# Gated DeltaNet inverse in a one-core transformer kernel: five doubling levels on TensorE against 16-row diagonal blocks on VectorE, through DRAM, and two levels

## The chip, the cores and the metric

The kernel runs on one core of one Trainium2 chip. The metric is the device time of one execution in microseconds; three runs of the kernel before are given. One more execution was taken by the hardware profiler, and every view below comes from it.

## What is computed

A block of a transformer on 256 tokens of width 2048 in float32: an input projection feeds two mixers, sparse attention and a Gated DeltaNet (GDN), which are gated and merged; an MLP, a second attention layer and a retention layer follow. The change is in the GDN. It has 8 heads of 128, and works on chunks of 64 tokens:

```
lower = where(strict, einsum('bhncd,bhnsd->bhncs', kb, k) * decay, 0)   # c = 64
tinv = triangular_solve(eye + lower, eye, lower=True, unit_diagonal=True)
u = tinv @ vb
w = tinv @ (kb * exp(g))
qk = einsum('bhncd,bhnsd->bhncs', q, k) * decay
# scan over the chunks
v_new = u_n - w_n @ state
o = (q_n * exp(g_n)) @ state + qk_n @ v_new
```

tinv is the inverse of a unit lower triangular 64 x 64 matrix, for 8 heads and 4 chunks.

## The kernel before

**The stream.** Nearly all time goes into projections. A job multiplies the 256 x 2048 activations with a 2048 x 512 block of weights, in 8 granules of 256 weight rows. Weights and activations are split into two float32r parts: ScalarE rounds a granule to w_hi (`split_hi`, L261), VectorE forms the rest, w_lo (`split_lo`, L269), TensorE does 8 matmuls with w_hi (L294) and 4 with w_lo (L300) on 512 columns. w_hi and w_lo have four slots each: `split_hi` of granule r waits until granule r - 4 is done. SyncE loads the weights 512 KB at a time into eight half-slots of raw, ahead of that.

**The slots.** The small work of the GDN is written as one generator per engine (`gdn_mix`), each cut into steps by `yield`. Before granule r, TensorE takes its next step; ScalarE and VectorE take theirs before they split granule r + 4. So step s of every engine lies beside granule s, and a step that waits holds back everything behind it on its engine, the splits too. Group 0 (heads 0 to 3) and group 1 (heads 4 to 7) follow one another, from the fifth GDN job (J_GDN + 4) on; up to the merge projections' end there are 12 jobs, 96 slots. A group takes 36 of them.

**The steps of a group.** On TensorE: 0 to 2 transpose the projected q, k and v of the group to columns; 3 and 4 the cumulated decay; 5 turns k back (`natural(0)`); 7 multiplies k with k; 11 transposes the tiles of A (L1608), 12 turns q (`natural(1)`, L1561); 13 to 22 are the levels of the inverse; 23 and 24 the products w (L1648) and u (L1654); 25 to 31 the scan over four chunks (L1666 to L1683); 35 turns the output (L340), for which VectorE's L2247 makes the last factor. VectorE does the taps of the convolution (`tap`, L2115, four instructions of 256 columns each), the decay matrix, at step 9 A = k k^T times decay and beta (L2166, semaphore a_ready), at step 10 the decay for q k^T and the gate z (L2169, L2172).

**The inverse.** All tiles have 128 x 128 elements, two chunks on the diagonal; 4 heads and 2 tiles make 8 tiles, processed by one instruction on VectorE and ScalarE (1024 columns) and eight on TensorE. Y is the transposed inverse of the diagonal blocks, which double in size at every level. Level 0 is Y = I - mask(0) * A^T (transposes L1608, then VectorE L2175 and L2177). Each of the levels 1 to 5 takes two slots:

```
P  = A^T Y  per tile    TensorE L1618, then transposes of Y, L1626
P1 = P * mask(l)        VectorE L2183;  X = copy of Y^T, ScalarE L1080
U  = X^T P1             TensorE L1633
Y  = Y - U              VectorE L2191
```

The k.q product (L1639) lies in the second slot of level 1, the turn of v (`natural(2)`) in that of level 5. The three taps of v's convolution are beside levels 2 to 4 on VectorE. A 128 x 128 float32 matmul has two records in the trace, a transpose one.

**GpSimd (POOL)** in this stretch only computes three reciprocal roots per group for the norms (`root_pool`, L429), of k, q and the output; it has loaded the masks before, and its other DMAs lie before or after the GDN. Its DMAs go through the queue q0; those of SyncE through q1.

**Memory.** The working tiles lie in one arena; g_nat, the projected heads in rows, is reused for the first four merge gates (`mg_a`), which ScalarE writes with a sigmoid at the end of each merge job.

## Time and profile before

| | us |
|---|---|
| runs (3) | 2828.3, 2831.04, 2833.46 |
| median | 2831.04 |
| profiled execution | 2830.05 |
| its span | 2828.2 |
| granted TensorE clock, mean | 0.995 |
| TensorE busy | 2781.5 |
| VectorE busy | 1606.9 |
| ScalarE busy | 1294.8 |
| GpSimd busy | 65.2 |

The span goes from the first to the last instruction of the profiled execution; some 2 us lie around it. PE is TensorE, PEld its weight loads, DVE is VectorE, ACT ScalarE, POOL GpSimd, SP SyncE. Times in timelines are microseconds from the start of the span. A matmul's duration overlaps the next one's, so the pitch of starts is what it costs.

### The profile page before, as it was taken

Reading aid. Unit: us, or ns where it says so; the run is one execution under the profiler, and the core shown is the slowest. Engines: PE = TensorE matmul, PEld = TensorE weight load, DVE = VectorE, ACT = ScalarE, POOL = GpSimd, SP = SyncE. Lnnn points to the kernel's source line nnn. Section 1 sums busy time; section 2 is a strip of 40 time slices with the busy share of each in tenths; the row PEclk is TensorE's granted clock in tenths of the full one; section 3 lists DMA queues with packets and bytes.
Section 4 is the critical chain, followed back from the end, with each engine's and each line's share of the span. In section 5 each row is a group of like instructions: output and inputs, shape, how many; then the busy total and the mean of one; then the engine's idle time right before and its main releaser. Section 6 shows DMA issues by size and latency. Waiting matters only on the chain.

```text
span 2828.2 us, 35643 instructions
## 1 busy us (share of the span) xinstructions
PE 2781.5 (98%) x13270; PEld 2316.4 (82%) x13270; DVE 1606.9 (57%) x1784; ACT 1294.8 (46%) x1606; POOL 65.2 (2%) x68
## 2 busy tenths in 40 slices
PE   8999999999999999999999999999999999999998
PEld 7878887888888888888888888888878888888887
DVE  5555757555655555555555656655565555555556
ACT  5554636444444444344444554445453434444442
POOL 1000000000000000000000000000000000000000
PEclk9999999999999999999999999999999999999999
DMA  8754534356667566666666587586655655666663
GB/s 240 243 164 142 148 105 138 115 151 193 208 203 193 189 195 185 190 190 187 193 186 186 164 163 171 170 161 161 217 171 169 191 168 188 196 175 183 177 211 123
DMA packets 259947, 502.23 MB, mean 178 GB/s; under 512 B 15880, under 2 KB 24360, under 8 KB 258784
## 3 DMA queue, kind: packets, MB, share of 16 engines
q1 hardware_dynamic: 256448, 486.73, 59.4%
q0 software_dynamic: 3200, 13.52, 1.9%
q8 instruction: 97, 1.59, 0.2%
q14 instruction: 42, 0.34, 0.0%
q10 hardware_dynamic: 160, 0.04, 0.0%
HBM read 496.56 MB, written 3.67 MB: 177 GB/s over the span
## 4 chain that ended last, share of the span: by engine, by line
PE 94%; DVE 2%; ACT 2%; issue 1%; DMA 0%; POOL 0%; ACTq 0%; DVEq 0%
PE acc L294 53%; PE acc L300 27%; PE mx L340 1%; PE acc L1734 1%; PE acc L1732 1%; PE acc L1733 1%; ACT w_hi L261 1%; ACT arena L503 1%; DVE w_lo L269 1%; PE mx L1618 1%; PE mx L1633 1%; PE mx L476 0%; PE mx L484 0%; PE mx L1626 0%; DMA res<-in_x 0%
## 5 line engine op out<-in xcount | busy, mean ns | idle before, releaser
L269 DVE TENSOR_TENSOR w_lo<-raw,w_hi 128x1024 fp32r<-128x1024 f32 x916 | 1123.5, 1228 | 1122.8 <-ACT w_hi L261 1109.7
L261 ACT ACTIVATE w_hi<-raw 128x1024 fp32r<-128x1024 f32 x916 | 971.1, 1061 | 1378.5 <-PE acc L300 1306.1
L294 PE MATMUL acc<-w_hi,lt_b_hi 128*128 128x512 f32 x1792 | 707.3, 395 | 0.0
L294 PE MATMUL acc<-w_hi,lt_b_lo 128*128 128x512 f32 x1792 | 698.0, 390 | 0.0
L294 PE MATMUL acc<-w_hi,lt_a_hi 128*128 128x512 f32 x1664 | 660.2, 397 | 0.0
L294 PE MATMUL acc<-w_hi,lt_a_lo 128*128 128x512 f32 x1664 | 651.1, 391 | 0.0
L300 PE MATMUL acc<-w_lo,lt_b_hi 128*128 128x512 f32 x1792 | 479.3, 389 | 0.0
L300 PE MATMUL acc<-w_lo,lt_a_hi 128*128 128x512 f32 x1664 | 446.8, 390 | 0.8 <-DVE w_lo L269 0.8
L294 PEld LDWEIGHTS acc<-w_hi,lt_b_lo 128*128 128x128 f32 x1792 | 337.0, 188 | 69.8 <-issue 1.9
L300 PEld LDWEIGHTS acc<-w_lo,lt_b_hi 128*128 128x128 f32 x1792 | 336.4, 188 | 70.3
L294 PEld LDWEIGHTS acc<-w_hi,lt_b_hi 128*128 128x128 f32 x1792 | 336.8, 188 | 69.7 <-issue 1.9
L300 PEld LDWEIGHTS acc<-w_lo,lt_a_hi 128*128 128x128 f32 x1664 | 313.6, 188 | 67.2 <-DVE w_lo L269 1.2
L294 PEld LDWEIGHTS acc<-w_hi,lt_a_hi 128*128 128x128 f32 x1664 | 314.2, 189 | 64.5 <-issue 1.0
L294 PEld LDWEIGHTS acc<-w_hi,lt_a_lo 128*128 128x128 f32 x1664 | 314.4, 189 | 62.8
L356 DVE TENSOR_TENSOR lt_a_lo<-mx,lt_a_hi 128x512 fp32r<-128x512 f32 (+1 forms) x64 | 41.2, 685 | 33.8 <-ACT lt_a_hi L348 33.8
L429 POOL TENSOR_TENSOR sm<-sm 128x2 f32<-128x2 f32 (+2 forms) x20 | 23.1, 1154 | 1610.6 <-DVE sm L423 825.0
L348 ACT ACTIVATE lt_a_hi<-mx 128x512 fp32r<-128x512 f32 (+1 forms) x64 | 34.7, 593 | 52.0 <-PE mx L340 52.0
L1732 PE MATMUL acc<-w_hi,lt_b_hi 128*128 128x512 f32 x128 | 50.1, 391 | 0.0
L1734 PE MATMUL acc<-w_hi,lt_b_lo 128*128 128x512 f32 x128 | 49.8, 389 | 0.0
L1733 PE MATMUL acc<-w_lo,lt_b_hi 128*128 128x512 f32 x128 | 49.8, 389 | 0.0
L340 PE MATMUL mx<-ident,arena 128*128 128x128 f32 x280 | 36.4, 273 | 2.9 <-DVE arena L2247 2.9
L340 PEld LDWEIGHTS mx<-ident,arena 128*128 128x128 f32 x280 | 32.5, 140 | 8.1 <-DVE arena L2247 3.8
(378 smaller groups left out, 1627.0 us busy)
## 6 DMA issues: line engine op xcount, KB each, us to landing
raw<-in_ret_w_in SPq DMA_DIRECT2D x192, 512.0 KB, 3.7
raw<-in_w_in SPq DMA_DIRECT2D x168, 512.0 KB, 3.6
raw<-in_w_up SPq DMA_DIRECT2D x128, 512.0 KB, 3.7
raw<-in_w_down SPq DMA_DIRECT2D x128, 512.0 KB, 4.5
raw<-in_fox_w_in SPq DMA_DIRECT2D x128, 512.0 KB, 4.5
raw<-in_ret_w_out SPq DMA_DIRECT2D x64, 512.0 KB, 3.9
raw<-in_w_o SPq DMA_DIRECT2D x32, 512.0 KB, 4.6
raw<-in_fox_w_out SPq DMA_DIRECT2D x32, 512.0 KB, 4.6
```

What stands on the lines that cost most here:

```text
L261: nc.scalar.activation(w_hi[:, r % 4], raw[:, slot, 2 * half:2 * half + 2, :], ACT.Copy).then_inc(hi_ready, 1)
L269: nc.vector.tensor_tensor(w_lo[:, r % 4], raw[:, slot, 2 * half:2 * half + 2, :], w_hi[:, r % 4].bitcast(F32), ALU.subtract) \
L294: nc.tensor.matmul(acc[par][t][:, :], lt[p][:, kt, t * P:(t + 1) * P], w_hi[:, r % 4, k, :], start=(kt == 0 and p == 0), stop=False)
L300: last = nc.tensor.matmul(acc[par][t][:, :], lt[0][:, kt, t * P:(t + 1) * P], w_lo[:, r % 4, k, :], start=False, stop=(kt == KT - 1))
L340: last = nc.tensor.transpose(mx[:, b % 4, (2 * c + t) * P:(2 * c + t + 1) * P], src(2 * b + c, t), ident[:, :])
L348: nc.scalar.activation(dst(b)[0], mx[:, b % 4, :].rearrange("p (c s) -> p c s", s=S), ACT.Copy).then_inc(lt_hi_ready, 1)
L356: nc.vector.tensor_tensor(lo, mx[:, b % 4, :].rearrange("p (c s) -> p c s", s=S), hi.bitcast(F32), ALU.subtract).then_inc(lt_lo_ready, 1)
L503: last = nc.scalar.activation(sc[:, j, a:b], sc[:, j, a:b], ACT.Exp, bias=rowmax[:, t, j:j + 1], accum_out=esum[:, t, j:j + 1])
L1618: last = MM(tile(2, h, t), g_A[:, h, t, :], g_Y[:, h, t, :], start=True, stop=True)
L1732: MM(o, a_hi, w_hi[:, r % 4, k, :], start=(kt % 8 == 0), stop=False)
L1733: MM(o, a_hi, w_lo[:, r % 4, k, :], start=False, stop=False)
L1734: last = MM(o, a_lo, w_hi[:, r % 4, k, :], start=False, stop=(kt % 8 == 7))
```

## The change

Levels 1 to 3 and the first Y of the old scheme (blocks of 1 to 16 rows) go. Instead each 16 x 16 diagonal block of A is put on one partition: 8 blocks in a tile of 128 rows, 8 tiles, so 64 partitions with 256 elements. When A is ready, POOL stores the eight tiles' diagonal 32 x 32 blocks to DRAM in four DMAs (rows of 128 bytes), clears g_Y, waits for the landing and loads the 16 x 16 blocks into g_low in two DMAs (rows of 64 bytes). VectorE inverts all 64 blocks at once by back substitution, k from 15 to 1, with two chained instructions per k, 30 in all, over three steps. POOL stores the 64 results in one DMA of 1 KB per partition, waits, and writes them to the diagonal of g_Y in eight DMAs (rows of 64 bytes). TensorE then does two levels, 16 to 32 and 32 to 64 rows, as before.

Around it the steps are laid out anew. A group has 40 slots instead of 36, and 16 of the 96 are left free at the end instead of 24. On TensorE step 11 is empty, 12 turns q, 14 is the k.q product, 19 turns v, 23 to 26 are the two levels, 27 and 28 w and u; everything from there on is four steps later. On VectorE 11 to 13 are the three taps of v, 14 to 16 the inversion, 17 qkT, 18 the squares of q, 20 the product of v and beta. ScalarE's silu of v is at step 15. Group 1 now starts in slot 40, where g_nat is still wanted, so the first merge job's sigmoid is written after granule 5 of the second merge job (`merge_gate`), and the tiles of `mg_b` lie in other places.

```diff
-LEVELS = 6
+BASE = 16
+LEVELS = 2
...
+        NBLK = P // BASE * HG * NT
+        g_low = at(4112, BASE, BASE)[0:NBLK]
+        g_inv = at(4112 + BASE * BASE, BASE, BASE)[0:NBLK]
+        g_one = at(4112 + BASE * BASE, BASE * BASE)[0:NBLK, ::BASE + 1]
+        g_tmp = at(4112 + 2 * BASE * BASE, BASE * BASE)[0:NBLK]
...
-        mg_b = at(4096, 4, NT, NB)
+        mg_b = [at(i, NT, NB) for i in (0, 3072, 4096, 5120)]
...
+        low_dram = nc.dram_tensor("low_blocks", [4, HG * NT, 32, 32], F32).ap()
+        inv_dram = nc.dram_tensor("inverted_blocks", [2, 4, HG * NT, BASE, BASE], F32).ap()
...
+            def gdn_root(g, n, i):
+                root_pool(pool, sg("gss_ready"), 3 * g + n + 1, gss[:, i].rearrange("p t h -> p (t h)"),
+                          grs[:, i].rearrange("p t h -> p (t h)"), NT * HG, sg("grs_ready"))
+
             for g in range(2):
-                for n, i in enumerate((0, 1, 0)):
-                    root_pool(pool, sg("gss_ready"), 3 * g + n + 1, gss[:, i].rearrange("p t h -> p (t h)"),
-                              grs[:, i].rearrange("p t h -> p (t h)"), NT * HG, sg("grs_ready"))
+                gdn_root(g, 0, 0)
+                pool.wait_ge(sg("a_ready"), g + 1)
+                a_tiles = g_A[:, :, :, :].rearrange("p h t c -> p (h t) c")
+                y_tiles = g_Y[:, :, :, :].rearrange("p h t c -> p (h t) c")
+                for q in range(4):
+                    r = slice(32 * q, 32 * q + 32)
+                    pool.dma_start(low_dram[q].rearrange("a r c -> r a c"), a_tiles[r, :, r]) \
+                        .then_inc(sg("blocks_stored"), 16)
+                ch.link(nc.gpsimd.memset(g_Y[:, :, :, :], 0.0))
+                pool.wait_ge(sg("conv_done"), 3 * g + 2)
+                pool.wait_ge(sg("blocks_stored"), 80 * g + 64)
+                for half in range(2):
+                    r = slice(BASE * half, BASE * half + BASE)
+                    load(g_low[32 * half:32 * half + 32], low_dram.rearrange("q a r c -> (q a) r c")[:, r, r],
+                         "low_loaded")
+                pool.wait_ge(sg("inv_ready"), g + 1)
+                pool.dma_start(inv_dram.rearrange("f q a r c -> (f q a) r c"), g_inv) \
+                    .then_inc(sg("blocks_stored"), 16)
+                pool.wait_ge(sg("blocks_stored"), 80 * g + 80)
+                for q in range(4):
+                    for half in range(2):
+                        r = slice(32 * q + BASE * half, 32 * q + BASE * half + BASE)
+                        load(y_tiles[r, :, r], inv_dram[half, q].rearrange("a r c -> r a c"), "inv_loaded")
+                gdn_root(g, 1, 1)
+                gdn_root(g, 2, 0)
...
-                for l in range(1, LEVELS):
-                    act.wait_ge(sg("inv_x"), 5 * g + l)
+                yield
+                yield
+                silu(2)
+                for _ in range(8):
+                    yield
...
+            def merge_gate(J, dst):
+                take(act, J, J % 2, lambda t: A(dst[:, t, :], acc[J % 2][t][:, :], ACT.Sigmoid, scale=by_rstd(t)))
+
+            split_job(split_hi, act, J_MERGE, mix)
+            for r in range(GPJ):
+                step(mix)
+                split_hi(act, J_MERGE + 1, r + 4, r + 5)
+
+                if r == 5:
+                    merge_gate(J_MERGE, mg_a[:, 0])
...
-                pe.wait_ge(sg("a_ready"), g + 1)
+                yield
+                natural(1)
+                yield
+                yield
+                pe.wait_ge(sg("gsq_ready"), 2 * g + 2)
                 for h in range(HG):
                     for t in range(NT):
-                        last = TR(tile(2, h, t), g_A[:, h, t, :], ident[:, :])
-                last.then_inc(sg("inv_p"), 1)
-                yield
-                natural(1)
-                yield
-
-                for l in range(1, LEVELS):
-                    pe.wait_ge(sg("inv_y"), LEVELS * g + l)
+                        ts = slice(t * P, (t + 1) * P)
+                        last = MM(tile(0, h, t), g_k[:, h, ts], g_q[:, h, ts], start=True, stop=True)
+                last.then_inc(sg("gram_ready"), 1)
+                for _ in range(5):
+                    yield
+                pe.wait_ge(sg("qkT_ready"), g + 1)
+                natural(2)
+                for _ in range(4):
+                    yield
+
+                for l in range(LEVELS):
+                    if l == 0:
+                        pe.wait_ge(sg("inv_loaded"), 128 * (g + 1))
+                        pe.wait_ge(sg("a_ready"), g + 1)
+                    else:
+                        pe.wait_ge(sg("inv_y"), LEVELS * g + l)
                     for h in range(HG):
                         for t in range(NT):
                             last = MM(tile(2, h, t), g_A[:, h, t, :], g_Y[:, h, t, :], start=True, stop=True)
                     last.then_inc(sg("inv_p"), 1)
-                    if l == 1:
-                        pe.wait_ge(sg("gsq_ready"), 2 * g + 2)
-                    if l == 2:
-                        pe.wait_ge(sg("qkT_ready"), g + 1)
+                    if l == 0:
+                        pe.wait_ge(sg("vb_ready"), g + 1)
                     for h in range(HG):
                         for t in range(NT):
                             last = TR(tile(0, h, t), g_Y[:, h, t, :], ident[:, :])
                     last.then_inc(sg("inv_x"), 1)
                     yield
                     pe.wait_ge(sg("inv_p1"), LEVELS * g + l + 1)
-                    pe.wait_ge(sg("inv_x_copied"), 5 * g + l)
+                    pe.wait_ge(sg("inv_x_copied"), LEVELS * g + l + 1)
                     for h in range(HG):
                         for t in range(NT):
                             last = MM(tile(2, h, t), g_X[:, h, t, :], g_P1[:, h, t, :], start=True, stop=True)
                     last.then_inc(sg("inv_u"), 1)
-                    if l == 1:
-                        for h in range(HG):
-                            for t in range(NT):
-                                ts = slice(t * P, (t + 1) * P)
-                                last = MM(tile(0, h, t), g_k[:, h, ts], g_q[:, h, ts], start=True, stop=True)
-                        last.then_inc(sg("gram_ready"), 1)
-                    if l == LEVELS - 1:
-                        natural(2)
...
-                dve.wait_ge(sg("inv_p"), LEVELS * g + 1)
-                TT(g_P1[:, :, :, :], high_ps, mask(0), ALU.mult).then_inc(sg("inv_p1"), 1)
-                dve.wait_ge(sg("inv_p1"), LEVELS * g + 1)
-                TT(g_Y[:, :, :, :], heads_bcast(heads_bcast(ident[:, :], NT), HG), g_P1[:, :, :, :], ALU.subtract) \
-                    .then_inc(sg("inv_y"), 1)
-                yield
-                yield
-                for l in range(1, LEVELS):
+                tap(2, 1)
+                yield
+                tap(2, 2)
+                yield
+                ch.link(nc.vector.memset(g_inv, 0.0))
+                ch.link(nc.vector.memset(g_one, 1.0))
+                tap(2, 3)
+                yield
+                dve.wait_ge(sg("low_loaded"), 32 * (g + 1))
+                for k in range(BASE - 1, 0, -1):
+                    n = BASE - k
+                    row = bcast(g_low[:, k, 0:k], n)
+                    known = heads_bcast(g_inv[:, k, k:BASE], k)
+                    prod = g_tmp[:, 0:k * n].rearrange("p (a b) -> p a b", b=n)
+                    ch.link(TT(prod, row, known, ALU.mult))
+                    last = TT(g_inv[:, 0:k, k:BASE], g_inv[:, 0:k, k:BASE], prod, ALU.subtract)
+                    if k > 1:
+                        ch.link(last)
+                    else:
+                        last.then_inc(sg("inv_ready"), 1)
+                    if k in (11, 6):
+                        yield
+                yield
+                dve.wait_ge(sg("gram_ready"), 3 * g + 3)
+                TT(g_qkT[:, :, :, :], low_ps, g_qkT[:, :, :, :], ALU.mult).then_inc(sg("qkT_ready"), 1)
+                yield
+                sum_squares(1)
+                yield
+                yield
+                dve.wait_ge(sg("gnat_turned"), 3 * g + 3)
+                TT(g_vb[:, :, :, :], nat_ps, bcast(tg[:, T_V], HD), ALU.mult).then_inc(sg("vb_ready"), 1)
+                yield
+                yield
+                yield
+                for l in range(LEVELS):
                     dve.wait_ge(sg("inv_p"), LEVELS * g + l + 1)
                     TT(g_P1[:, :, :, :], high_ps, mask(l), ALU.mult).then_inc(sg("inv_p1"), 1)
-                    if l == 1:
-                        sum_squares(1)
-                    if l in (2, 3, 4):
-                        tap(2, l - 1)
-                    yield
-                    dve.wait_ge(sg("inv_u"), 5 * g + l)
-                    dve.wait_ge(sg("inv_y"), LEVELS * g + l)
+                    yield
+                    dve.wait_ge(sg("inv_u"), LEVELS * g + l + 1)
+                    if l:
+                        dve.wait_ge(sg("inv_y"), LEVELS * g + l)
                     TT(g_Y[:, :, :, :], g_Y[:, :, :, :], high_ps, ALU.subtract).then_inc(sg("inv_y"), 1)
-                    if l == 1:
-                        dve.wait_ge(sg("gram_ready"), 3 * g + 3)
-                        TT(g_qkT[:, :, :, :], low_ps, g_qkT[:, :, :, :], ALU.mult).then_inc(sg("qkT_ready"), 1)
-                    yield
-                dve.wait_ge(sg("gnat_turned"), 3 * g + 3)
+                    yield
                 nc.vector.memset(g_o[0:CHUNK, 0, :, :], 0.0)
-                TT(g_vb[:, :, :, :], nat_ps, bcast(tg[:, T_V], HD), ALU.mult).then_inc(sg("vb_ready"), 1)
...
-        b = 2 ** lv
+        b = BASE * 2 ** lv
```

TensorE, at the point where a group's inverse begins, before (L1618 is the first product of a level, L1626 the transposes of Y; L300 ends the granule ahead of them, L294 begins the next):

```order
L300 MATMUL acc<-w_lo,lt_a_hi 128x512 x3
L1618 MATMUL mx<-arena 128x128 [waits inv_y]
L1618 MATMUL mx<-arena 128x128 x7
L1626 MATMUL mx<-ident,arena 128x128 [waits gsq_ready]
L1626 MATMUL mx<-ident,arena 128x128 x7
L294 MATMUL acc<-w_hi,lt_a_hi 128x512 [waits hi_ready]
```

and the same point after, where the lines are L1677 and L1683:

```order
L301 MATMUL acc<-w_lo,lt_a_hi 128x512 x3
L1677 MATMUL mx<-arena 128x128 [waits a_ready,inv_loaded]
L1677 MATMUL mx<-arena 128x128 x7
L1683 MATMUL mx<-ident,arena 128x128 [waits vb_ready]
L1683 MATMUL mx<-ident,arena 128x128 x7
L295 MATMUL acc<-w_hi,lt_a_hi 128x512 [waits hi_ready]
```

It now stands at step 23 and not 13, and waits for the DMAs (inv_loaded) where it waited for VectorE's Y.

VectorE after, from step 13 (the two clears and the last tap of v) to the first operations of the inversion (L2237 the product, L2238 the subtraction; dve_step is the chain's semaphore):

```order
L2227 MEMSET arena 64x256
L2228 MEMSET arena 64x16 [waits dve_step]
L2164 SCALAR_TENSOR_TENSOR arena<-arena,cwg 128x256 [waits dve_step]
L2164 SCALAR_TENSOR_TENSOR arena<-arena,cwg 128x256 x3
L270 TENSOR_TENSOR w_lo<-raw,w_hi 128x1024 [waits hi_ready]
L2237 TENSOR_TENSOR arena<-arena 64x15 [waits low_loaded]
L2238 TENSOR_TENSOR arena<-arena 64x15 [waits dve_step]
L2237 TENSOR_TENSOR arena<-arena 64x28 [waits dve_step]
L2238 TENSOR_TENSOR arena<-arena 64x14x2 [waits dve_step]
```

Ten such operations stand between two w_lo. Before, steps 11 and 12 held L2175 and L2177 here, and then the levels.

POOL after, between the first root of a group and the next two (in the kernel before the three roots stand side by side):

```order
L430 TENSOR_TENSOR sm<-sm 128x8 [waits gss_ready]
L841 DMA low_blocks<-arena 32x8x32 [waits a_ready]
L841 DMA low_blocks<-arena 32x8x32 x3
L843 MEMSET arena 128x1024
L784 DMA arena<-low_blocks 32x16x16 [waits blocks_stored,conv_done,pool_step]
L784 DMA arena<-low_blocks 32x16x16
L851 DMA inverted_blocks<-arena 64x256 [waits inv_ready]
L784 DMA arena<-inverted_blocks 16x8x16 [waits blocks_stored]
L784 DMA arena<-inverted_blocks 16x8x16 x7
L430 TENSOR_TENSOR sm<-sm 128x8 [waits gss_ready] x3
```

Fifteen DMAs per group have come in between. The last row covers the two roots left of this group and the first of the next.

## Rows read from the trace of the kernel before

**Rows 1.** The page: busy time by engine, and the chain that ended last.
```profile
PE 2781.5 (98%) x13270; PEld 2316.4 (82%) x13270; DVE 1606.9 (57%) x1784; ACT 1294.8 (46%) x1606; POOL 65.2 (2%) x68
...
PE 94%; DVE 2%; ACT 2%; issue 1%; DMA 0%; POOL 0%; ACTq 0%; DVEq 0%
```

**Rows 2.** Waits of TensorE, 295 to 640 us: who, for whom, us, times, longest.
```profile
PE mx L340 <- DVE arena L2247: 2.9, 2, 1.5
...
PE mx L1618 <- DVE arena L2177: 1.6, 2, 1.2
```

**Rows 3.** TensorE timeline after the GDN: start, us, engine, line, instruction.
```profile
606.54 1.07 PE L300 MATMUL acc<-w_lo,lt_a_hi 128*128 128x512 f32 x4
...
609.26 1.07 PE L300 MATMUL acc<-w_lo,lt_a_hi 128*128 128x512 f32 x4
```

**Rows 4.** TensorE timeline, levels of group 0 and the w products.
```profile
357.14 1.95 PE L1618 MATMUL mx<-arena 128*128 128x128 f32 x16
...
362.56 1.95 PE L1633 MATMUL mx<-arena 128*128 128x128 f32 x16
...
367.10 1.95 PE L1618 MATMUL mx<-arena 128*128 128x128 f32 x16
...
397.83 1.95 PE L1648 MATMUL mx<-arena 128*128 128x128 f32 x16
```

**Rows 5.** TensorE timeline, step 11 of group 0.
```profile
336.65 1.09 PE L1608 MATMUL mx<-ident,arena 128*128 128x128 f32 x8
```

**Rows 6.** TensorE timeline, steps 11, 12 and 23 of group 1.
```profile
490.64 1.04 PE L1608 MATMUL mx<-ident,arena 128*128 128x128 f32 x8
...
494.26 1.04 PE L1561 MATMUL mx<-ident,arena 128*128 128x128 f32 x8
...
551.00 1.95 PE L1648 MATMUL mx<-arena 128*128 128x128 f32 x16
```

**Rows 7.** VectorE timeline, steps 7 to 11 of group 0.
```profile
326.04 1.22 DVE L269 TENSOR_TENSOR w_lo<-raw,w_hi 128x1024 fp32r<-128x1024 f32 x1
327.18 1.67 DVE L2115 SCALAR_TENSOR_TENSOR arena<-arena,cwg 128x256 f32<-128x256 f32 x4
328.88 0.17 DVE L2157 TENSOR_TENSOR tg<-tok,sm 128x8 f32<-128x8 f32 x1
329.08 0.17 DVE L2158 TENSOR_TENSOR tg<-tg,sm 128x8 f32<-128x8 f32 x1
...
335.38 1.22 DVE L2166 TENSOR_TENSOR arena<-mx,arena 128x1024 f32<-128x1024 f32 x1
...
342.76 1.22 DVE L2175 TENSOR_TENSOR arena<-mx,arena 128x1024 f32<-128x1024 f32 x1
```

**Rows 8.** POOL timeline at the start: issues, with the idle time before them.
```profile
37.49 0.54 POOL L801 DMA_DIRECT2D sm<-in_dt_bias  x1
...
40.14 1.11 POOL L805 DMA_DIRECT2D bias_by_distance<-arena  x1
75.61 1.81 POOL L810 DMA_DIRECT2D arena<-bias_by_distance  x2 [34.36 <-DMA bias_by_distance<-arena]
```

**Rows 9.** DMA view: issues by line, KB each, median us to landing.
```profile
bias_by_distance<-arena POOLq DMA_DIRECT2D x1, 1536.0 KB, 35.2
...
out_x<-res SPq DMA_DIRECT2D x4, 256.0 KB, 2.1
...
arena<-c_masks POOLq DMA_DIRECT2D x1, 512.0 KB, 4.9
...
arena<-in_w_in POOLq DMA_DIRECT2D x1, 128.0 KB, 8.4
...
arena<-in_fox_w_in POOLq DMA_DIRECT2D x1, 128.0 KB, 14.8
...
arena<-c_masks POOLq DMA_DIRECT2D x1, 64.0 KB, 3.8
```

**Rows 10.** Stretch 307 to 460 us: busy us per engine, clock, DMA share, GB/s.
```profile
307.00:460.00 153.00, 150.37 (x873) 129.18 (x872) 100.05 (x134) 73.55 (x98) 5.85 (x3) 1.00 0.43 124
```

20 lines of the change are left out of this document (11 added, 9 removed).

## The prediction

> **What bounds the kernel now.** I read the page first. The profiled execution took 2830.05 us, of which 2828.2 us is the span; the median of the three runs shown is 2831.04 us. TensorE is busy for 98% of the span, and the chain that ended last is 94% TensorE [rows 1]. So an instruction taken from TensorE's stream counts in full, as long as nobody else is late. Then I asked who waited for whom on TensorE between 295 and 640 us, the part with both groups of the GDN. Of its waits two bear on the change: 2.9 us at the transposes of the output (L340), and 1.6 us before the first level of the inverse, where VectorE forms the first Y (L2177) [rows 2]. All else there is work.
>
> What does that work cost? A slot of the interleaving is one granule of the big projection plus what a step puts in front of it. The bare granule is the pitch of the L300 groups after the GDN, 609.26 - 606.54 = 2.72 us [rows 3]. One level of the inverse takes two slots, from the L1618 at 357.14 to the next at 367.10, 9.96 us; less two granules (5.44) it is 4.52 us of small matmuls. The half with L1633 alone is 367.10 - 362.56 - 2.72 = 1.82 us [rows 4]. A slot with eight transposes lasts from L1608 at 490.64 to L1561 at 494.26, 3.62 us [rows 6], so 0.90 us above a granule.
>
> **The change on TensorE.** I count from step 11 of a group, the transposes of A at L1608, to the w products at L1648. Before: 336.65 to 397.83 = 61.18 us in group 0 and 490.64 to 551.00 = 60.36 us in group 1, twelve slots each [rows 4 to 6]. Less 12 x 2.72 = 32.64 us, the small work and its wait are 28.54 and 27.72 us. After, the same stretch has sixteen slots. What stands ahead of their granules: q and v transposes, 2 x 0.90; the k.q product in a slot of its own, 1.82 (as many matmuls as L1633); two levels, 2 x 4.52. That is 12.66 us. The gain is 15.9 + 15.1 = **31.0 us**. It is mostly three levels out of five, twice (27.1), then the transposes of A (1.8) and what was waited for L2177. The four extra slots of a group are no loss: the granules are the same 96, and these are taken from the 24 that had nothing beside them; 16 remain.
>
> **What is added, and the room it has.** Three things lie beside TensorE: VectorE's 30 small operations per group, a trip of the blocks of A through DRAM, and a trip of the inverses back. TensorE's clock: the slots from 336.65 on add up to 2.72 + 3.62 + 2.72 + 4.54 + 4 x 2.72 + 3.62 + 3 x 2.72 = 36.3 us, so step 23, which waits for inv_loaded, begins at 372.9.
>
> VectorE's clock: L2166 makes a_ready at 335.38 + 1.22 = 336.6. Up to 342.76, where L2175 stood, nothing changes. Then three taps come with a w_lo each: a tap is 328.88 - 327.18 = 1.70 us, a w_lo 327.18 - 326.04 = 1.14 [rows 7], in all 8.5, and two memsets, which I estimate at 0.5 together from the pitch of small operations and their 272 elements. So VectorE comes to the wait for low_loaded at 351.8, **15.2 us** after a_ready. A chained operation on 8 elements starts 0.20 us after the one before it [rows 7]; for up to 64 elements, at a w_lo's 1.14 us per 1024, I take 0.22. Ten are 2.2 us; three tens and two w_lo between them are 8.9 us. inv_ready then falls at 360.7, and trip 2 has **12.2 us** before TensorE asks.
>
> Does the burst itself starve TensorE? VectorE's slots there are 1.14 + 2.2 = 3.3 us against 2.72, but it works four granules ahead. The w_lo behind the first ten belongs to granule 18, whose lo matmuls come after 8 of its 12, 1.8 us into it, at 360.2. The tightest is granule 20's, at 366.5, behind all thirty and three w_lo (10.0 us): low_loaded may come as late as 356.5, 19.9 us after a_ready. So there are 4.7 us of room, and the excess of three slots is 1.9. Cost zero; the room would be used up at 0.38 us per operation. Behind the wait for low_loaded on VectorE the w_lo of the next granules are queued, so a late one first eats the 4.7 us and then stops TensorE at L301.
>
> **Trip 1:** four issues on POOL, then two loads behind their semaphore. A POOL issue takes 0.54 us for 128 pieces and 1.11 for 1024 [rows 8]; I take 0.75 for these of 256 and 0.8 for 512. Landing counts from the start of the issue: the bias store, issued at 40.14 and landed after 35.2 us, was followed at 75.61, which puts 0.27 us on the wake-up [rows 8, 9]. Loads on POOL's queue landed after 3.8 us (64 KB of masks), 4.9 (1024 pieces of masks), 8.4 and 14.8 (2048 pieces of 64 bytes); SyncE's stores of 256 KB after 2.1 [rows 9]. For the stores, 1024 pieces in all, I take 4.9, for the 1024 pieces of 64 bytes half of 14.8: 3 x 0.75 + 4.9 + 0.27 + 0.8 + 7.4 = 15.6 us. Bounds: 2.1 and 3.8 give 9.2, 8.4 and 14.8 give 26.5.
> **Trip 2:** one store of 64 rows of 1 KB, eight issues of 128 pieces. 3.8 + 0.27 + 7 x 0.54 + 3.8 = 11.7 us, with the 64 KB row as the nearest in size; bounds 10.0 (2.1 and 3.8) and 27.3 (8.4 and 14.8).
> Where trip 1 is longer than 15.2, the stall per group is (trip 1 + trip 2) - (15.2 + 12.2). With 15.6 + 11.7 it is just nothing: **0 us**, with hardly any to spare. By the Trainium skill, DMA: Bandwidth & Descriptors, section Anatomy of one DMA — SWDGE (gpsimd) path, a DMA costs about 2.0 us and its bytes over 436e3; both trips would then be about 8 us, the stall surely nothing, and the sum below the same. No row on this queue is that short.
>
> Edits with one answer. POOL's memset of g_Y runs while the stores land; without that cover it would be one more operation in trip 1. The roots of q and of the output wait behind trip 2's eight issues; the first is wanted at step 27, four after inv_loaded. The 3136 more pieces per group go to DMA engines that are 43% busy [rows 10], and the weights have eight half-slots; if that cover went, w_hi would wait for raw. The sigmoid of the first merge job moves by six granules; its accumulators are wanted after eight. Silu of v at step 15 follows its last tap by two steps. All zero.
>
> **Sum:** 2830.05 - 31.0 + 0 = 2799.1 us for the profiled execution, 2800.0 against the median. I leave 0.5 us for a wait in one of the trips: **2800.5 us**.
>
> **Rivals.** *Small pieces are slow (12%).* Both trips load 1024 pieces of 64 bytes, and such a load took 14.8 us. Against it: the equal one of w_in landed after 8.4, and both had 2048 pieces [rows 9]. With 8.4 in all four places the trips are 20.1 and 20.9, the stall 13.6 us per group, and the time 2827; with a stall of 8 it is 2816; at both upper bounds, 26 us, 2853.
> *Short stores are read first (5%).* If each 128-byte piece costs a read and a write, the stores take 2 x 4.9, trip 1 is 20.5, the stall 4.8 us per group and the time 2810. No store in such pieces is in this trace. By the Trainium skill, same page, section Specifications, a transfer below 512 B does read-modify-write.
> *The store pays per piece (5%), slower than before.* The one store on POOL's queue took 35.2 us for 1024 pieces [rows 9], and the blocks leave in 1024 pieces. Then trip 1 is 35.2 + 0.27 + 0.8 + 7.4 = 43.7 us and the stall 43.7 + 11.7 - 27.4 = 28 us per group: + 56 - 31, 2856 us, with VectorE held at L2237 and TensorE at L301. The time crosses that of before when the two trips reach 43 us together. Against it: those pieces had 1536 bytes and came from 8 partitions, these have 128 and come from 32.
> *VectorE becomes the bound (3%).* With 0.5 us per chained operation the thirty take 8.4 us more, the stall is about 8 us per group, 2817. The pitch of 0.20 speaks against it [rows 7].
> *Nothing is gained (3%)*, because ScalarE or VectorE sets the pace of the slots: 2831. Against it is how little TensorE waits [rows 2].
>
> **Numbers.** About 0.2% (5.7 us) is what a measurement can tell from no change. The forecast has 72%. Of the first rival 9 of 12 parts end below 2825.4. Faster: 0.72 + 0.09 + 0.05 + 0.03 = 0.89; same 0.03 + 0.03 = 0.06; slower 0.05. The range starts at 2797, where the 2.9 us at L340 goes too, and ends at 2813, a stall of 6 us per group; about 5% lie below and 14% above.
>
> **What would show it.** L1677 with L1683, and L1690, stand twice per group; the stretch to the w products holds 12.7 us beside its sixteen granules; no wait above 1 us is put to a DMA or to low_blocks; the thirty operations have a pitch of 0.20 to 0.25 us; low_blocks lands within 5 us and its loads within 8. It would be wrong if TensorE waits at L1677 for a DMA, at L301 for a w_lo behind L2237, or if w_hi waits for raw.

## The result and the profile after

The changed kernel takes 2804.92 us (median of 4 runs, 2802.91 to 2805.71); the kernel before, timed beside it, 2831.53 us (4 runs). The ratio is 0.9906, interval 0.9892 to 0.992: faster, by 26.6 us. The forecast was 2800.5 us with a range of 2797 to 2813. The profiled execution took 2804.46 us, and my sum for it was 2799.1: it promised 31.0 us, and 25.6 came.

The page, as in [rows 1], with its lines on the busy time and the chain:

```profile
PE 2753.8 (98%) x13014; PEld 2288.1 (82%) x13014; DVE 1599.7 (57%) x1832; ACT 1285.3 (46%) x1598; POOL 83.6 (3%) x100
...
PE 93%; DVE 3%; ACT 2%; issue 1%; DMA 0%; POOL 0%; ACTq 0%; DVEq 0%
```

TensorE is busy for 27.7 us less, more than the 25.6 us that the time fell. So the matmuls went as planned, and something was given back. The chain says where to look: VectorE's share rose from 2% to 3%. The waits of TensorE between 295 and 640 us, the view of [rows 2] (who, for whom, us, times, longest):

```profile
PE mx L1608 <- DVE arena L2247: 3.9, 2, 1.9
PE mx L341 <- DVE arena L2315: 2.9, 2, 1.5
PE mx L1608 <- ACT arena L1072: 1.4, 1, 1.4
```

L341 is the old L340 and waits as before. The other two are new. L1608 is now the line of `natural`; L2247 is qkT, the decay times k.q, which VectorE makes at step 17 (not the L2247 of [rows 2], which has become L2315); L1072 is ScalarE's silu, the old L1038. The wait for L2177 has gone with its level. So has a third wait of the kernel before, which [rows 2] does not show, at the turn of k in group 1:

```profile
PE mx L1561 <- ACT arena L1038: 1.7, 1, 1.7
```

The same on TensorE's timeline (start, us, engine, line, instruction, idle time before it). First the stretch that I use as a ruler from here on, from a group's first transposes to the output turn of group 1, before:

```profile
298.19 1.09 PE L1552 MATMUL mx<-ident,res 128*128 128x128 f32 x8
...
601.04 1.09 PE L340 MATMUL mx<-ident,arena 128*128 128x128 f32 x8 [1.46 <-DVE arena L2247]
```

and after, with the steps of group 0 and the places in group 1 that matter:

```profile
298.05 1.09 PE L1599 MATMUL mx<-ident,res 128*128 128x128 f32 x8
...
363.06 1.09 PE L1608 MATMUL mx<-ident,arena 128*128 128x128 f32 x8 [1.93 <-DVE arena L2247]
...
374.90 1.95 PE L1677 MATMUL mx<-arena 128*128 128x128 f32 x16
...
384.86 1.95 PE L1677 MATMUL mx<-arena 128*128 128x128 f32 x16
...
489.94 1.10 PE L1608 MATMUL mx<-ident,arena 128*128 128x128 f32 x8 [1.36 <-ACT arena L1072]
...
513.86 1.09 PE L1608 MATMUL mx<-ident,arena 128*128 128x128 f32 x8 [1.93 <-DVE arena L2247]
...
515.11 0.63 PE L295 MATMUL acc<-w_hi,lt_a_lo 128*128 128x512 f32 x1
...
518.10 1.20 PE L301 MATMUL acc<-w_lo,lt_a_hi 128*128 128x512 f32 x4
...
527.32 0.94 PE L1677 MATMUL mx<-arena 128*128 128x128 f32 x7
```

A level with its two granules takes 384.86 - 374.90 = 9.96 us, to the hundredth what it took in [rows 4]. The inverse is asked for at 374.90, where I had 372.9: the 1.93 us of the wait lie between. In group 1 the same wait has a tail. The eight matmuls of L295 behind it start 0.43 us apart and last 0.63, where they normally start 0.23 apart and last 0.39. So from the turn of v to the first level, 11.84 us pass in group 0 (363.06 to 374.90) and 13.46 in group 1 (513.86 to 527.32): 1.62 us more. It is the granted clock of TensorE; the windows of that place (busy us of PE, PEld, DVE, ACT, POOL, then the granted clock, DMA share, GB/s):

```profile
509.00:514.00 5.00, 3.07 (x14) 2.22 (x14) 4.69 (x14) 2.12 (x2) 0.56 (x1) 1.00 0.46 123
514.00:517.00 3.00, 3.00 (x14) 2.50 (x14) 2.97 (x4) 0.00 (x0) 2.95 (x6) 0.65 0.85 214
517.00:520.00 3.00, 3.00 (x12) 2.40 (x11) 0.40 (x1) 0.61 (x1) 2.92 (x4) 0.78 0.91 250
520.00:523.00 3.00, 3.00 (x14) 2.45 (x14) 2.36 (x2) 1.32 (x2) 0.00 (x0) 1.00 0.25 85
```

Full clock up to the wait's end, 0.65 and 0.78 behind it, full again from 520 us. By the pitches this is half speed for some 3.5 us, the lower of the two levels, 1.2 instead of 2.4 GHz.

Why is qkT late? VectorE's timeline around the inversion, which answers to [rows 7]:

```profile
335.19 1.22 DVE L2215 TENSOR_TENSOR arena<-mx,arena 128x1024 f32<-128x1024 f32 x1
...
351.52 0.16 DVE L2237 TENSOR_TENSOR arena<-arena 64x15 f32<-64x15 f32 x1
351.71 0.18 DVE L2238 TENSOR_TENSOR arena<-arena 64x15 f32<-64x15 f32 x1
...
355.90 0.22 DVE L2237 TENSOR_TENSOR arena<-arena 64x64 f32<-64x64 f32 x1
356.15 0.22 DVE L2238 TENSOR_TENSOR arena<-arena 64x64 f32<-64x64 f32 x1
...
360.57 0.17 DVE L2238 TENSOR_TENSOR arena<-arena 64x15 f32<-64x15 f32 x1
360.66 1.21 DVE L270 TENSOR_TENSOR w_lo<-raw,w_hi 128x1024 fp32r<-128x1024 f32 x1
361.80 1.21 DVE L2247 TENSOR_TENSOR arena<-mx,arena 128x1024 f32<-128x1024 f32 x1
```

A_ready comes at 335.19 + 1.22 = 336.41 (forecast 336.6), the burst starts at 351.52 (351.8) without idle time before it, the thirty operations end at 360.57 + 0.17 = 360.74 (360.7). Behind them stand one more w_lo and then qkT, 1.14 + 1.22 us, until 363.0. TensorE asked at 363.06 - 1.93 = 361.13.

The trips through DRAM on POOL's timeline, group 0 (count of DMAs after the x):

```profile
336.71 2.38 POOL L841 DMA_DIRECT2D low_blocks<-arena  x4 [10.14 <-DVE arena L2215]
339.08 0.98 POOL L843 MEMSET arena<- 128x1024 f32 x1
341.00 1.30 POOL L784 DMA_DIRECT2D arena<-low_blocks  x2 [0.94 <-DMA low_blocks<-arena]
361.03 0.57 POOL L851 DMA_DIRECT2D inverted_blocks<-arena  x1 [18.73 <-DVE arena L2238]
363.25 4.21 POOL L784 DMA_DIRECT2D arena<-inverted_blocks  x8 [1.65 <-DMA inverted_blocks<-arena]
```

and in the DMA view from 320 to 380 us (KB each, median us from issue to landing), as [rows 9]:

```profile
low_blocks<-arena POOLq DMA_DIRECT2D x4, 32.0 KB, 2.0
arena<-inverted_blocks POOLq DMA_DIRECT2D x8, 8.0 KB, 2.9
arena<-low_blocks POOLq DMA_DIRECT2D x2, 32.0 KB, 2.3
inverted_blocks<-arena POOLq DMA_DIRECT2D x1, 64.0 KB, 1.9
```

An issue takes 0.53 to 0.65 us. Trip 1 is 341.00 + 0.65 + 2.3 - 336.41 = 7.5 us; VectorE comes for it 7.6 us later. In trip 2 the median of 2.9 us hides a spread. For both groups together the view of this tensor gives, from issue to landing:

```profile
DMA to landing us min/median/max: 1.9/2.9/4.4
```

The last load is what counts. In group 0 it is issued at 363.25 + 7 x 0.53 = 367.0 and lands 3.6 us later, at 370.6: 9.8 us after the burst's end, and 2.4 us before an undelayed TensorE would ask (374.90 - 1.93 = 372.97). In group 1 it is issued at 517.7 and lands 4.4 us later, 10.6 us after the burst's end; an undelayed TensorE would ask at 527.32 - 1.93 - 1.62 = 523.8, 1.7 us later. No wait is put to a DMA.

**Ledger of the stretch.** The stretch is 601.04 - 298.19 = 302.85 us with 71 granules before, and 597.26 - 298.05 = 299.21 with 79. Less 2.72 us a granule, 109.73 and 84.33 us lie beside the granules: a gain of 25.40 us. From the stretch's end to the end of the span it is 2227.16 us before and 2205.34 + 8 x 2.72 = 2227.10 after, so nothing else changed. Of the 31.0 us promised: - 3.86 for qkT, - 1.62 for the clock, - 1.36 for L1072, + 1.73 for the wait of the old kernel at the turn of k in group 1 (for ScalarE's L1038), which I had not counted and which is gone. That makes 25.9; 0.5 us is unexplained.

### The profile page after: what moved, and what is told of

Its sections match the earlier page's. It is cut to its first block, busy times and chain, and to the rows that moved or that the text cites. A ratio compares the mean times of both kernels' runs of the same rounds, so it can differ in the third digit from the quotient of the medians.

```text
span 2802.6 us, 35198 instructions
## 1 busy us (share of the span) xinstructions
PE 2753.8 (98%) x13014; PEld 2288.1 (82%) x13014; DVE 1599.7 (57%) x1832; ACT 1285.3 (46%) x1598; POOL 83.6 (3%) x100
## 4 chain that ended last, share of the span: by engine, by line
PE 93%; DVE 3%; ACT 2%; issue 1%; DMA 0%; POOL 0%; ACTq 0%; DVEq 0%
PE acc L295 53%; PE acc L301 26%; PE mx L341 1%; DVE w_lo L270 1%; PE acc L1783 1%; PE acc L1782 1%; PE acc L1781 1%; ACT w_hi L262 1%; ACT arena L504 1%; PE mx L477 0%; DVE arena L2164 0%; PE mx L485 0%; DMA res<-in_x 0%; PE mx L1861 0%; PE acc L2001 0%
## 5 line engine op out<-in xcount | busy, mean ns | idle before, releaser
L295 PE MATMUL acc<-w_hi,lt_b_hi 128*128 128x512 f32 x1792 | 706.9, 394 | 0.0
L295 PE MATMUL acc<-w_hi,lt_b_lo 128*128 128x512 f32 x1792 | 697.8, 389 | 0.0
L295 PE MATMUL acc<-w_hi,lt_a_hi 128*128 128x512 f32 x1664 | 660.2, 397 | 0.0
L295 PE MATMUL acc<-w_hi,lt_a_lo 128*128 128x512 f32 x1664 | 651.9, 392 | 0.0
L295 PEld LDWEIGHTS acc<-w_hi,lt_b_lo 128*128 128x128 f32 x1792 | 336.6, 188 | 69.8 <-issue 1.9
L295 PEld LDWEIGHTS acc<-w_hi,lt_b_hi 128*128 128x128 f32 x1792 | 336.5, 188 | 69.9 <-issue 1.9
L295 PEld LDWEIGHTS acc<-w_hi,lt_a_hi 128*128 128x128 f32 x1664 | 314.5, 189 | 65.2 <-issue 1.0
L295 PEld LDWEIGHTS acc<-w_hi,lt_a_lo 128*128 128x128 f32 x1664 | 314.8, 189 | 63.2
L341 PE MATMUL mx<-ident,arena 128*128 128x128 f32 x280 | 36.4, 273 | 2.9 <-DVE arena L2315 2.9
L341 PEld LDWEIGHTS mx<-ident,arena 128*128 128x128 f32 x280 | 32.5, 140 | 8.1 <-DVE arena L2315 3.8
```

The costliest lines, as they stand in the source:

```text
L295: nc.tensor.matmul(acc[par][t][:, :], lt[p][:, kt, t * P:(t + 1) * P], w_hi[:, r % 4, k, :], start=(kt == 0 and p == 0), stop=False)
L341: last = nc.tensor.transpose(mx[:, b % 4, (2 * c + t) * P:(2 * c + t + 1) * P], src(2 * b + c, t), ident[:, :])
```

## The experiments

My theory: 31.0 us was right as the value of the matmuls, and what is missing is one wait, TensorE's for qkT behind the burst on VectorE, with the clock that falls behind it. Rivals: the levels left are worth less than 4.52 us; the thirty operations cost by themselves, wherever qkT stands; the trips through DRAM cost in a way that is not put down as a wait.

All results in one table. "Beside" is the ruler: the stretch less 2.72 us per granule; by the forecast it would be 109.73 - 31.0 = 78.7 us for the change. Three sets were timed, each beside the kernel before: "changed" (before: 2831.53 us), the four from "changed, again" to "a third level" (2833.38), and the last four (2829.94). The kernel before differs by 3.4 us between the sets, so times of different sets are compared by their ratios or by the stretch.

| kernel | median us (lowest, highest) | ratio to before, interval | stretch | granules | beside |
|---|---|---|---|---|---|
| before | 2831.53; 2833.38; 2829.94 | 1 | 302.85 | 71 | 109.7 |
| changed | 2804.92 (2802.91, 2805.71) | 0.9906 (0.9892, 0.992) | 299.21 | 79 | 84.3 |
| changed, again | 2805.52 (2803.81, 2805.9) | 0.9901 (0.9886, 0.9917) | 299.25 | 79 | 84.4 |
| qkT ahead of the burst | 2803.16 (2799.27, 2804.11) | 0.9888 (0.9873, 0.9903) | 294.43 | 79 | 79.6 |
| v turned a slot later | 2798.57 (2797.72, 2800.5) | 0.9879 (0.9863, 0.9894) | 293.32 | 79 | 78.4 |
| a third level | 2817.2 (2808.99, 2819.79) | 0.9942 (0.9928, 0.9955) | 319.20 | 83 | 93.4 |
| burst left out | 2798.76 (2798.27, 2801.0) | 0.989 (0.9873, 0.9906) | 293.29 | 79 | 78.4 |
| three turns a slot later | 2795.23 (2791.55, 2796.53) | 0.988 (0.9863, 0.9896) | 293.70 | 81 | 73.4 |
| levels a slot earlier | 2800.37 (2798.87, 2806.46) | 0.9894 (0.9878, 0.9911) | 288.61 | 77 | 79.2 |
| v turned a slot earlier | 2813.07 (2810.62, 2814.79) | 0.9943 (0.9927, 0.996) | 306.79 | 79 | 91.9 |

### The changed kernel once more

No edit.

> The changed kernel once more, on the chip of the runs beside it. Theory A (the qkT wait): the forecast missed 4.4 us because TensorE, about to turn v (L1608, step 19), waits 1.93 us per group for VectorE's qkT product (L2247), which the 30 small operations have pushed back; and in group 1 the granted clock fell to 0.65 for some 4 us right after that wait, which cost 1.7 us more. Then this run shows 1.9 us twice at L1608 again and 2804.9 us within 2 us; whether the clock falls again after a wait of that size is open. Rival B (traffic): the missing time is the DMA traffic and POOL's writes beside TensorE; then the slow granules need not follow the wait.

The stretch is 299.25 us against 299.21, with the same three waits. The clock fell again behind the wait in group 1, and not in group 0. So the stretch repeats within 0.04 us, while the medians of the whole differ by 0.6; I judge by the stretch where a few us matter.

### qkT ahead of the burst

```diff
                 yield
+                dve.wait_ge(sg("gram_ready"), 3 * g + 3)
+                TT(g_qkT[:, :, :, :], low_ps, g_qkT[:, :, :, :], ALU.mult).then_inc(sg("qkT_ready"), 1)
                 dve.wait_ge(sg("low_loaded"), 32 * (g + 1))
...
                 yield
-                dve.wait_ge(sg("gram_ready"), 3 * g + 3)
-                TT(g_qkT[:, :, :, :], low_ps, g_qkT[:, :, :, :], ALU.mult).then_inc(sg("qkT_ready"), 1)
                 yield
```

> VectorE forms the qkT product before the inversion instead of after it; all else as changed. Theory A: no wait at L1608 in step 19 for VectorE, no fall of the clock there, 3.9 to 5.7 us less than the changed kernel, 2799 to 2801 us. The inversion ends 1.2 us later, and TensorE's step 23 still finds inv_loaded done (it had about 3 us left, of which it loses 1.9 by starting earlier and 1.2 by the later end, so a wait of up to 0.5 us is possible). Rival B: the time stays at 2804.9.

Waits of TensorE, 295 to 640 us:

```profile
PE mx L341 <- DVE arena L2315: 2.9, 2, 1.5
PE mx L1608 <- ACT arena L1072: 1.4, 1, 1.4
PE mx L1677 <- DMA arena<-inverted_blocks: 0.5, 1, 0.5
```

The wait for qkT is gone, the clock stays up in the stretch, and the stretch is 4.78 us shorter (3.86 + 1.62 = 5.48 less the new 0.5 would be 4.98). The new line shows how thin the room of trip 2 is: qkT's 1.2 us ahead of the burst make the inverse later by as much, the last load takes up to 5.3 us to land here, and TensorE, no longer held up before, reaches L1677 half a us before it has landed.

The whole time moved only 2.4 us, from 2805.52 to 2803.16, and stayed above the 2799 to 2801 us that were expected. Part of the rest went at 746 us, where TensorE waits for a w_lo that VectorE makes late, since VectorE waits there for x to be loaded again: 9.62 us in this kernel, 8.30 in the changed one. TensorE's timeline:

```profile
746.52 1.20 PE L301 MATMUL acc<-w_lo,lt_a_hi 128*128 128x512 f32 x4 [2.16 <-DVE w_lo L270]
...
747.84 0.63 PE L295 MATMUL acc<-w_hi,lt_a_lo 128*128 128x512 f32 x1
```

In the changed kernel that wait is 0.83 us and the matmuls behind it are at full speed. Before the GDN this execution was also 3.2 us behind that of the next kernel (the stretch begins at 299.19 against 296.02), with a fall of the clock near 150 us. Neither place is touched by the edit.

### v turned a slot later

On TensorE `natural(2)` goes from step 19 to 20, on VectorE v times beta from 20 to 21; nothing else moves.

```diff
-                for _ in range(5):
+                for _ in range(6):
                     yield
...
                 natural(2)
-                for _ in range(4):
+                for _ in range(3):
                     yield
...
                 yield
+                yield
                 dve.wait_ge(sg("gnat_turned"), 3 * g + 3)
...
                 yield
-                yield
                 yield
```

> TensorE turns v one slot later (step 20), VectorE's product with beta one step later too; VectorE's order of the inversion and qkT is as changed. Theory A: the wait is gone as well, since qkT is ready at 363.0 and step 20 begins at 363.8: 2799 to 2801 us, the same as with qkT first. Rival B: 2804.9. Rival C (VectorE's burst costs TensorE elsewhere, through late w_lo): this one stays slower than with qkT first or both stay above 2801.

Stretch of the timeline (the first transposes and the output turn of group 1):

```profile
296.02 1.09 PE L1599 MATMUL mx<-ident,res 128*128 128x128 f32 x8
...
589.34 1.09 PE L341 MATMUL mx<-ident,arena 128*128 128x128 f32 x8 [1.46 <-DVE arena L2315]
```

It is 293.32 us, 5.89 less than the changed kernel's: the 3.86 us of the wait, the 1.62 of the clock, and 0.4. Beside the granules lie 78.4 us, where the forecast had 78.7. The whole time is 7.0 us shorter (2805.52 to 2798.57). Theory confirmed: the order of two steps was worth 6 us. It settles the third rival too: both trips through DRAM are still there, and the whole 31 us are there as well, so the trips cost nothing, put down as a wait or not.

### A third level

`LEVELS = 3`, with an empty mask for the level added, so that it does a level's work and changes nothing:

```diff
-LEVELS = 2
+LEVELS = 3
...
-        masks.append((c // (2 * b) == s // (2 * b)) & (c // b + 1 == s // b))
+        masks.append((c // (2 * b) == s // (2 * b)) & (c // b + 1 == s // b) & (b < CHUNK))
```

> One more level per group on TensorE, with an empty mask, so that the result stays and the work is 24 small matmuls and transposes in two more slots (42 per group). It prices the main term of the forecast, 4.52 us per level: the changed kernel and 9.0 us, 2813.9. If part of a level were hidden, it would be 4 to 8 us more; if the changed kernel's slots are paced by another engine, less than 4.

Less four granules more (10.88), the stretch, from the transposes at 293.33 to the output turn at 612.53, is 308.32 us, 9.11 more than the changed kernel's; two levels at 4.52 are 9.04. Within it two things cancel: the clock did not fall, - 1.6, and ScalarE's L1072 was waited for twice in group 1, at the turn of k and at that of q, + 1.5:

```profile
473.79 1.06 PE L1608 MATMUL mx<-ident,arena 128*128 128x128 f32 x8 [1.73 <-ACT arena L1072]
...
496.87 1.09 PE L1608 MATMUL mx<-ident,arena 128*128 128x128 f32 x8 [1.12 <-ACT arena L1072]
```

A level taken away is worth what the pitch says; that rival falls. The whole time differs by 11.7 us on the medians, and is 3.3 us above what was expected; the spread is the widest of all kernels here, 2809 to 2820. The profiled execution is the fastest of the five, 2808.99 us at a mean granted clock of 0.997; the others took 2813.65 to 2819.79 us at 0.993 to 0.995. No trace of these is kept, so where the 2.6 us beyond the stretch lie stays open.

### The burst left out

Of the thirty operations only the last is left, which keeps the order. The kernel leaves the inversion out, so its inverses are wrong values; the trips and TensorE's stream stay.

```diff
-                    ch.link(TT(prod, row, known, ALU.mult))
-                    last = TT(g_inv[:, 0:k, k:BASE], g_inv[:, 0:k, k:BASE], prod, ALU.subtract)
-                    if k > 1:
-                        ch.link(last)
-                    else:
-                        last.then_inc(sg("inv_ready"), 1)
+                    if k == 1:
+                        TT(g_inv[:, 0:k, k:BASE], g_inv[:, 0:k, k:BASE], g_low[:, 0:1, 1:BASE], ALU.subtract) \
+                            .then_inc(sg("inv_ready"), 1)
```

> The 30 small operations of VectorE per group are left out but for one that keeps the order, so the inverses are wrong values; the trips, the waits and TensorE's stream are as in the changed kernel. Theory A: qkT is then ready before TensorE wants it, and TensorE gains what the v turn's later slot gave: the GDN stretch (from the first L1599 to the second group's output transposes) goes from 299.2 to 293.3 us, the time to 2799. Rival C (VectorE's burst costs TensorE more than this one wait): the stretch falls below 292.

The stretch is 293.29 us, within 0.03 of the kernel that keeps all thirty operations and turns v a slot later. So the burst costs nothing but what stands behind it: with qkT out of TensorE's way, its 6.9 us on VectorE (360.74 - 351.52, less two w_lo of 1.14) are free. The rival that the operations cost by themselves falls.

### Three turns a slot later

v as above, and also the turn of q and the output turn one slot later, a group of 41 slots: the places of the two other waits.

```diff
                 yield
+                yield
                 squares(1)
-                yield
                 yield
...
                 yield
+                yield
                 natural(1)
-                yield
                 yield
...
                 yield
+                yield
                 pe.wait_ge(sg("go_ready"), g + 1)
...
```

Left out of this cut are the edit of the section on v, and one more `yield` on ScalarE and on VectorE, so that their groups have 41 steps too.

> v turned one slot later, and the two other waits of the stretch treated alike: q turned one slot later (it waited 1.4 us for ScalarE in group 1) and the output one slot later (1.46 us for L2315 in each group); 41 slots per group. Theory A: each slot moved back costs nothing, because the granules are the same, so the waits are the gain: 4.3 us below the kernel with v turned later, 2794.3 us; the stretch, two granules (5.4 us) longer, 294.5. If a wait is only moved on to the next work, the time stays at 2798.6.

```profile
296.25 1.09 PE L1600 MATMUL mx<-ident,res 128*128 128x128 f32 x8
...
589.95 1.04 PE L341 MATMUL mx<-ident,arena 128*128 128x128 f32 x8
```

In this kernel the view of TensorE's waits between 295 and 640 us is empty. 73.4 us lie beside the granules, 5.1 less than with v alone moved; the waits taken away were 4.3, and 0.8 is open. In its set it is the fastest, 2795.23 us, 3.5 less than with the burst left out. But its ratio, 0.988, is that of v alone turned later, 0.9879: by the whole time the two cannot be told apart, by the stretch they can. Against the changed kernel's 0.9901 and 0.9906 the intervals just overlap. It costs two of the sixteen free slots.

### The levels a slot earlier

v turned a slot later and everything from the levels on a slot earlier, 39 slots, so that trip 2 has 2.7 us less:

```diff
-                for _ in range(5):
+                for _ in range(6):
                     yield
...
                 natural(2)
-                for _ in range(4):
+                for _ in range(2):
                     yield
...
```

ScalarE and VectorE have one `yield` less before their levels (left out of the cut).

> As with v turned later, but the two levels begin one slot earlier (39 slots per group). It measures the room of the second trip: with v turned later the last inverse was issued at 364.9 and, at the 4.8 us from issue to landing that the short wait in the kernel with qkT first shows, landed at 369.7, 1.0 us before step 23 at 370.7. One slot less then makes TensorE wait 1.7 us per group at L1677 for the DMA: 3.4 us more than with v turned later, 2802; up to 3.5 more if the clock falls after these waits. If the landing is the 2.9 us of the DMA view, there is no wait and 2798.6.

TensorE's timeline at the first level of each group:

```profile
372.77 2.05 PE L1677 MATMUL mx<-arena 128*128 128x128 f32 x16 [0.38 <-DMA arena<-inverted_blocks]
...
518.60 2.05 PE L1677 MATMUL mx<-arena 128*128 128x128 f32 x16 [1.21 <-DMA arena<-inverted_blocks]
```

and POOL's, the store of the inverses in each:

```profile
363.22 0.57 POOL L851 DMA_DIRECT2D inverted_blocks<-arena  x1 [18.76 <-DVE arena L2238]
...
507.45 0.56 POOL L851 DMA_DIRECT2D inverted_blocks<-arena  x1 [18.81 <-DVE arena L2238]
```

Here TensorE ends its wait with the last landing, so this is the price of trip 2 that the changed kernel hides: 9.6 and 11.2 us from the store's issue, some 0.3 more from the end of the burst. The excess over the room is what shows as waits, 1.6 us in all, less than half of the 3.4 that were expected; in group 0 the last load landed after 3.6 us and in group 1 after 5.2, where 4.8 had been taken for both. The clock fell behind neither. One slot fewer buys nothing: beside the granules 79.2 us, 0.7 more than with v alone moved (+ 1.6 for the DMA, - 1.4 since the wait for L1072 is gone; 0.5 is open).

### v turned a slot earlier

```diff
-                for _ in range(5):
+                for _ in range(4):
                     yield
...
                 natural(2)
-                for _ in range(4):
+                for _ in range(5):
                     yield
```

> The suspected wait made larger: v is turned one slot earlier than in the changed kernel (step 18). Theory A: TensorE waits 1.9 + 2.7 = 4.6 us per group for VectorE's qkT, 5.4 us more in all, 2810; with a fall of the clock after each wait 1.7 us more in group 0, 2812. Rival B: 2804.9.

TensorE's timeline at the turn of v in group 0:

```profile
361.57 1.97 PE L1608 MATMUL mx<-ident,arena 128*128 128x128 f32 x8 [4.64 <-DVE arena L2247]
363.19 0.77 PE L295 MATMUL acc<-w_hi,lt_a_hi 128*128 128x512 f32 x1
...
363.76 0.63 PE L295 MATMUL acc<-w_hi,lt_a_lo 128*128 128x512 f32 x1
```

The wait goes from 1.93 to 4.64 us, by 2.71, a slot, in each group: the finishing time of qkT is fixed by VectorE, and TensorE waits the difference. The whole time, 2813.07 us, is 1 us above the higher of the two values expected. Now the clock falls behind both waits. The stretch is 7.58 us longer: 5.4 of waiting, and 2.2 of clock, which now falls in group 0 too and already during the transposes (1.97 us instead of 1.09).

## Why the prediction was right, and what it missed

**What bounds the kernel**: right. TensorE's stream counts in full: the third level cost 9.11 us for 9.04, and taking one wait away with the clock behind it gave 5.9 for 5.5. Wrong was "All else there is work": the same view had the 1.7 us for ScalarE's L1038.

**The change on TensorE, 31.0 us**: right as a value of the work: with v turned later, 109.7 - 78.4 = 31.3 us. For the change as it stands the run gave 25.4.

**TensorE's clock and VectorE's clock**: right to 0.3 us each where nothing waited (336.4 for 336.6, 351.5 for 351.8, 360.7 for 360.7). I took 0.22 us per small operation; the steps are 0.19 to 0.25. The last of the three agrees partly by luck: the burst began 0.3 us early and took 9.2 us where I had 8.9.

**The step that failed** is "Does the burst itself starve TensorE?", which ends in "Cost zero". It tested the burst against the w_lo queued behind it, granule by granule, and against inv_ready, but not against qkT, which step 17 puts behind the burst and for which TensorE's step 19 waits before it turns v. The numbers for it stood in the text. By my own clocks qkT is ready at 360.7 + 1.14 + 1.22 = 363.1; TensorE comes to step 19 at 336.65 + 2.72 + 3.62 + 2.72 + 4.54 + 4 x 2.72 = 361.1. That is 2.0 us per group; the trace has 1.93. Behind it the same step missed the clock: I had no term for it, and it cost 1.6 us in group 1. Together 5.5 of the 5.6 us by which the gain in the stretch fell short. That 2804.92 us still lies in the range is luck in this respect: its upper part stood for a stall of the trips, and none came.

**The turn of q**: costed as 0.90 us without a wait. In the old kernel the transposes of A at step 11 came ahead of it, 0.90 us of cover; these are gone, and in group 1 it waits 1.36 us for ScalarE. A wait of 1.73 us at the turn of k went away, which I had not counted either. It had held TensorE back ahead of the turn of q as well; how much of the 1.36 us each of the two accounts for was not separated. The 1.36 and the 1.73 nearly cancel, which is luck.

**The trips**: the stall of zero was right, trip 1 much too long. It took 7.5 us for 15.6, below even my lower bound of 9.2; trip 2 took 9.8 and 10.6 in the changed kernel, and 9.8 and 11.4 where TensorE waited for it, for 11.7. The error in trip 1 was to scale from the loads of [rows 9]: they had 128 and 512 KB, its loads have 32 and landed after 2.3 us (median), where I had 7.4. In trip 2 the store landed after 1.9 us for 3.8, and the last load after 3.6 and 4.4 for 3.8. By the Trainium skill, DMA: Bandwidth & Descriptors, section Anatomy of one DMA — SWDGE (gpsimd) path, a DMA costs about 2.0 us and hardly anything for so few bytes. The stores agree with that, with 2.0 and 1.9 us; the loads of trip 2 do not quite, with 1.9 to 4.4. The 8 us that the prediction made of it for each trip was the better term for trip 1, and too short for trip 2.

**The rivals**: none came. Loads of 32 KB in 64-byte pieces landed after 2.3 us, stores in 128-byte rows after 2.0; the store does not pay per piece at this size, and VectorE's operations take 0.19 to 0.25 us and not 0.5. The read-modify-write below 512 B that the Trainium skill states (DMA: Bandwidth & Descriptors, section Specifications) shows nowhere in these landings: the stores in 128-byte rows took 2.0 us, the store in 1 KB rows 1.9. Closest was "VectorE becomes the bound": VectorE did hold up TensorE, but by the order of its work, not by the price of an operation.

**The signs asked for**: two L1677 and two L1690 per group, no wait for a DMA, the pitch of the burst, blocks within 5 and 8 us: all there. That the stretch would hold 12.7 us beside sixteen granules was the one that failed, since the wait of 1.93 us lies in it, and the list of what would make me wrong did not have the wait that came.

## What to carry to other kernels

Where a burst is put into an in-order engine, write down every result that this engine makes behind it, and for each the time at which its reader asks; not only the ones that seem critical. Here one row in such a list, two steps apart in the program, was worth 6 us of 31, and moving the reader one slot removed it at no cost. And where a kernel lives at 98% of TensorE, compare variants over the stretch that changed: it repeated to 0.04 us, while the whole time moved by 2 to 3 us through places that no edit touched.

## What the runs showed of the hardware

**A wait can cost nearly double through the clock.** Behind some waits of TensorE the granted clock is at the lower level for a few us, though the engine has work at once: eight matmuls at a pitch of 0.43 instead of 0.23 us, 1.6 us in all. It came behind waits of 1.93 and 1.91 us (group 1, in two executions of the changed kernel), 2.16 and 4.64 us (twice). It did not come behind those of 1.93 and 1.91 in group 0 of the same executions, of 1.92 and 1.91 in the kernel with a third level, of 1.73, 1.46 and 1.36 us. So the same wait at the same length can have it or not. Nor does it need a wait: in the changed kernel the clock is 0.50 from 201 to 204 us, where TensorE waits for nobody; shortly ahead of the fall it works through matmuls of only 7 and 15 columns (L1536 and L1537). The first place outside the stretch shows this between two kernels that are the same up to there, qkT ahead of the burst:

```profile
150.21 2.65 PE L485 MATMUL mx<-ident,arena 128*128 128x128 f32 x12 [1.97 <-ACT arena L504]
```

and v turned a slot later, with the same transposes after the same wait at full speed:

```profile
148.85 1.50 PE L485 MATMUL mx<-ident,arena 128*128 128x128 f32 x12 [1.98 <-ACT arena L504]
```

That there are two levels, 1.2 and 2.4 GHz, is in the Trainium skill, TensorE: Matmul & The Clock Gate, Part 1: The HAM clock gate, and the granted clock of 1.00 and 0.50 here agrees; what decides which of two equal waits is followed by the lower one, these runs do not tell.

**Small DMAs through DRAM are cheap.** 32 KB in 128-byte pieces landed in 2.0 us, 8 KB in 64-byte pieces in 2.9 (medians; the second 1.9 to 4.4), with 169 GB/s moving in all between 320 and 380 us, nearly all of it weights. A whole trip, out in one piece and back in eight, was 9.8 to 11.4 us, nearly half of it POOL's issues at 0.53 us each.

**A chained operation on VectorE costs 0.19 us with 15 elements per partition and 0.25 with 64.** Thirty of them, 64 blocks at a time, took the place of three levels with 4.52 us of matmuls each on TensorE, and lay beside it. By the Trainium skill, VectorE: DVE Perf Modes, section The DRAIN you can't avoid, the semaphores between the operations of such a chain cost nothing extra, and it is their number that counts. The second half fits: four times the elements add only 0.06 us. The first no run here shows, since every operation of the burst has a semaphore behind it.
